# Start of a two-layer fp32 kernel: bias rows and modulation rows moved into the empty expert ring, the bias store moved to the first attention, the modulation's second part spread over the attention's units

## The reference, cut to what matters

```python
# second block, layer l; hc is the context, h the tokens that the first block gives
mod_c = (silu(c_ctx) @ w_mod[l] + b_mod[l])         # 6 rows of 1024; the same for c
cn = rms_norm(hc, norm1_g[l]) * (1 + mod_c[1]) + mod_c[0]
pc = cn @ w_in[l]                                   # q, k, v, pool, conv, gates
oc = diff_attn_core(qc, kc, vc, lam)                # 8 heads, 256 tokens: "attention 0"
hc = hc + mod_c[2] * mixer_output(oc, pc, ...)      # gates, pooling, convolution, w_out
cn2 = rms_norm(hc, norm2_g[l]) * (1 + mod_c[4]) + mod_c[3]
hc = hc + mod_c[5] * peer_ffn(cn2, ...)             # rows of 16384 experts, gathered
# first block, layer ab: s = q k^T + bias[bucket(distance)], bias from rel_bias (32 x 16)
```

## Time and profile before

| | |
|---|---|
| median of 3 runs | 4165.67 us |
| lowest and highest | 4165.25, 4172.52 us |
| span of the profiled execution (the page gives no other time of it) | 4175.5 us |
| PE, DVE, POOL busy | 50%, 67%, 45% of the span |
| mean granted TensorE clock | 0.734 of full speed |
| chain that ended last, by engine | PE 37%, DVE 27%, POOL 15%, issue 9%, DMA 7% |

### The profile page before, as it was taken

One profiled execution on the slowest core, in us unless ns is written; L12 is line 12 of the kernel. 1 busy time (PEld: TensorE's weight loads), 2 busy tenths in 40 slices (PEclk: granted clock), 3 DMA queues, 4 the chain that ended last, 5 costly groups with the idle time before them and its releaser, 6 DMA issues.

```text
span 4175.5 us, 29452 instructions
## 1 busy us (share of the span) xinstructions
PE 2101.5 (50%) x10122; PEld 1670.6 (40%) x10122; DVE 2787.7 (67%) x4546; ACT 414.1 (10%) x915; POOL 1893.4 (45%) x1556
## 2 busy tenths in 40 slices
PE   2798998637678578869435000009899800000000
PEld 0546887536467356767114000007688700000000
DVE  0104113996877997766987888994511399898898
ACT  0103001111311220011001000001400100000000
POOL 0000000355654776540875777770000057778776
PEclk7897999868788679989767555559999955555555
DMA  9552455779998989987998999993144557999999
GB/s 118 155 182 92 142 186 186 249 246 349 332 333 294 330 306 369 373 325 237 373 344 324 392 350 374 372 345 130 43 151 156 172 185 258 334 378 342 375 374 347
DMA packets 533813, 1140.12 MB, mean 273 GB/s; under 512 B 38125, under 2 KB 327789, under 8 KB 532878
## 3 DMA queue, kind: packets, MB, share of 16 engines
q0 software_dynamic: 224832, 814.87, 54.5%
q1 hardware_dynamic: 308832, 323.37, 23.6%
HBM read 1130.67 MB, written 7.44 MB: 273 GB/s over the span
## 4 chain that ended last, share of the span: by engine, by line
PE 37%; DVE 27%; POOL 15%; issue 9%; DMA 7%; ACT 2%; another core or an unknown queue 2%; SPq 0%; DVEq 0%; ACTq 0%; POOLq 0%
PE PS L399 35%; POOL ring L919 15%; DVE acc L1269 11%; DVE ring L1263 6%; DMA wring<-in_w_in 2%; DMA wring<-in_w_mod 1%; DMA ring<-in_peer_u,eidx 1%; ACT work L947 1%; DVE work L1323 1%; DVE work L1716 1%; DVE work L1714 1%; DVE work L1713 1%; PE PS L655 1%; DVE work L1329 1%
## 5 line engine op out<-in xcount | busy, mean ns | idle before, releaser
L919 POOL DMA_INDIRECT ring<-in_peer_u,eidx x768 | 996.9, 1298 | 1817.0 <-DVE small L1369 751.6
L919 POOL DMA_INDIRECT ring<-in_peer_v,eidx x768 | 885.3, 1153 | 431.4 <-issue 208.4
L1269 DVE SCALAR_TENSOR_TENSOR acc<-ring,small,acc 128x1024 f32<-128x1024 f32 x762 | 977.6, 1283 | 78.8 <-DMA ring<-in_peer_v,eidx 15.5
L1263 DVE SCALAR_TENSOR_TENSOR ring<-ring,xn_peer 128x1024 f32<-128x1024 f32 x768 | 930.5, 1219 | 122.4 <-DMA ring<-in_peer_u,eidx 114.1
L399 PE MATMUL PS<-wring,xnT 128*128 128x256 f32 (+1 forms) x3360 | 749.2, 387 | 43.9 <-issue 35.1
L399 PEld LDWEIGHTS PS<-wring,xnT 128*128 128x128 f32 x3360 | 651.2, 196 | 140.0 <-issue 40.9
L399 PE MATMUL PS<-xnT,wring 128*128 128x128 f32 (+1 forms) x2896 | 482.1, 329 | 30.6 <-DMA wring<-in_w_in 15.0
L399 PEld LDWEIGHTS PS<-xnT,wring 128*128 128x128 f32 x2896 | 439.8, 195 | 71.9 <-DMA wring<-in_w_in 16.6
L407 PE MATMUL PS<-const,work 128*128 128x128 f32 (+1 forms) x358 | 60.4, 334 | 744.6 <-DVE work L1326 681.0
L407 PEld LDWEIGHTS PS<-const,work 128*128 128x128 f32 (+1 forms) x358 | 52.0, 170 | 753.2 <-DVE work L1326 685.8
L947 ACT ACTIVATE work<-PS 128x512 f32<-128x512 f32 (+7 forms) x391 | 201.6, 535 | 1392.9 <-PE PS L399 1144.6
(11 more groups left out here) (151 smaller groups left out, 1484.9 us busy)
## 6 DMA issues: line engine op xcount, KB each, us to landing
wring<-in_w_in SPq DMA_DIRECT2D x128, 1024.0 KB
wring<-in_w_mod SPq DMA_DIRECT2D x48, 1024.0 KB
wring<-in_peer_wq SPq DMA_DIRECT2D x48, 1024.0 KB
wring<-in_ab_w_in SPq DMA_DIRECT2D x13, 1024.0 KB
wring<-in_conv_out_w SPq DMA_DIRECT2D x12, 1024.0 KB
wring<-in_w_out SPq DMA_DIRECT2D x12, 1024.0 KB
ring<-in_peer_u,eidx POOLq DMA_INDIRECT x768
ring<-in_peer_v,eidx POOLq DMA_INDIRECT x768
```

The lines of the kernel that those rows point to most:

```text
L919: pool.indirect_dma_start(ring[:, m % NG, :], None, table, bass.IndirectOffsetOnAxis(ap=eidx[:, r % 2, t, k:k + 1], axis=0))\
L1263: v.scalar_tensor_tensor(out=slot, in0=slot, scalar=1.0, in1=xn_peer[:, t, :], op0=ALU.mult, op1=ALU.mult, accum_out=hid[:, k:k + 1]).then ...
L1269: v.scalar_tensor_tensor(out=acc[:, :], in0=slot, scalar=wgt[:, k - NSEL:k - NSEL + 1], in1=acc[:, :], op0=ALU.mult, op1=ALU.add).then_inc ...
```

## The change

`MODROW` of layer 0, `hot` and `brow` move from `work` to `ring`, so that nothing of mixer 0 lies under them. The constants are split: the pooling matrices come as their own load, on SP ahead of the block ("mod0_1", 0), with a semaphore of their own, for which PE waits before the pooling. `modulation(0, 1)` is no longer called in one piece: PE runs one of its 8 units after the scores of each odd unit of attention 0, and ACT copies its rows in the next step. POOL waits for the first scores of attention 0, then loads `x`, then stores the bias rows. SP loads the norm row and the first two q blocks ahead of the first `mod_out`, and the second `mod_out` moves from g0 to u. ACT's waits for `bias_stored` and `mod_stored` go; POOL gets one for `mod_stored` ahead of the experts. ACT copies `xnT` ahead of the exponentials of lambda.

```diff
-        MODROW = [[work[0:2, b:b + 2 * D] for b in base] for base in ((0, 8192, 14336), (0, 2048, 4096))]
-        hot = work[0:33, 12288:13312].rearrange("p (g j) -> p g j", g=2)
-        brow = work[0:8, 13312:14336].rearrange("p (g j) -> p g j", g=2)
+        early = ring[:, :, :].rearrange("p n d -> p (n d)")
+        MODROW = [[early[0:2, b:b + 2 * D] for b in (0, 2048, 4096)], [work[0:2, b:b + 2 * D] for b in (0, 2048, 4096)]]
+        hot = early[0:33, 6144:7168].rearrange("p (g j) -> p g j", g=2)
+        brow = early[0:8, 7168:8192].rearrange("p (g j) -> p g j", g=2)
...
-            def attention(s, units, scores, turns, values):
+            def attention(s, units, scores, turns, values, between=None):
...
                         done(ins, "S", s, u)
+                        if between:
+                            between(u)
...
-                qkv(r, "qkv", (lambda: modulation(0, 1)) if r == 0 else None)
+                qkv(r, "qkv")
...
-                attention(r, M_UNITS, scores, turns, values)
+                def modulate(u):
+                    if u % 2:
+                        modulation(0, 1, u // 2)
+
+                attention(r, M_UNITS, scores, turns, values, modulate if r == 0 else None)
...
+                pe.wait_ge(poolm_landed, 16)
                 for c in range(0, KD, 2):
...
-            sp.dma_start(const[:, :], DR["const"]).then_inc(const_landed, 16)
+            sp.dma_start(const[:, 0:C_POOL], DR["const"][:, 0:C_POOL]).then_inc(const_landed, 16)
...
+            def load_pool_matrices():
+                sp.dma_start(const[:, C_POOL:C_ALL], DR["const"][:, C_POOL:C_ALL]).then_inc(poolm_landed, 16)
...
-                ("q0", 0): [(mod_out, 0, 0, 1), (load_rows, "n1_0", "sc_0", "sh_0", "ag_0"), (load_smalls, 0)],
-                ("g00", 0): [(mod_out, 0, 1, 3), (load_rows, "ps_0", "m2_0")],
+                ("q0", 0): [(load_rows, "n1_0")],
+                ("q0", 2): [(mod_out, 0, 0, 1), (load_rows, "sc_0", "sh_0")],
+                ("k0", 0): [(load_smalls, 0), (load_rows, "ag_0")],
+                ("mod0_1", 0): [(load_pool_matrices,)],
+                ("u0", 0): [(mod_out, 0, 1, 3), (load_rows, "ps_0", "m2_0")],
...
-            pool.dma_start(H["x"][:, :, :], DR["x"][0].rearrange("(t p) d -> p t d", p=P)).then_inc(x_landed, 16)
             slow(cT[:, :, 0], DR["c_2"][0].rearrange("(k p) -> p k", p=P), c_landed)
...
+            pool.wait_ge(*at("product", "S", 0, 0))
+            pool.dma_start(H["x"][:, :, :], DR["x"][0].rearrange("(t p) d -> p t d", p=P)).then_inc(x_landed, 16)
             for g in range(2):
                 pool.wait_ge(*at("read", "bias", g))
...
             pool.wait_ge(bias_stored, 32)
+            pool.wait_ge(mod_stored, 48)
...
-                if r == 0:
-                    act.wait_ge(bias_stored, 32)
                 for n in names:
...
-                    if r == 0 and n == "v":
-                        modulation(0, 1)
...
-                if r == 0:
-                    act.wait_ge(mod_stored, 48)
...
                 norm(("m", r), H[s], before)
+                norm_turn(("m", r))
                 if r in (0, 3):
                     act.wait_ge(*at("lam_dots", r))
                     A(act.activation(lam2[:, :], lam2[:, :], ACT.Exp), "lam_exp", r)
-                norm_turn(("m", r))
...
                 for u in range(len(M_UNITS) + 2):
+                    if r == 0 and u and u % 2 == 0:
+                        modulation(0, 1, 4 + u // 2 - 1)
```

More of the change, by code:

```diff
@@ L41 @@
 C_FREQ = C_IOTA + 16
-C_POOL = C_FREQ + 16
-C_ONES = C_POOL + 4 * T * S
-C_ALL = C_ONES + 2
+C_ONES = C_FREQ + 16
+C_POOL = C_ONES + 2
+C_ALL = C_POOL + 4 * T * S
 def constants():
@@ L62, in constants @@
     c[:, C_IOTA:C_IOTA + 16] = np.arange(16)
-    c[:, C_ONES:C_ALL] = 1.0
+    c[:, C_ONES:C_POOL] = 1.0
     c[:, C_FREQ:C_FREQ + 16] = 10000.0 ** (-np.arange(0, C_ROPE, 2) / C_ROPE)
@@ L248, in program @@
         freq = const[:, C_FREQ:C_FREQ + 16]
-        poolm = const[:, C_POOL:C_ONES].rearrange("p (i t s) -> p i t s", i=4, t=T)
+        poolm = const[:, C_POOL:C_ALL].rearrange("p (i t s) -> p i t s", i=4, t=T)
         O_TOK, PROB = wk(10240, T, D), [wk(12288, 1024), wk(13312, 1024)]
@@ L301, in program @@
         slot_used = sem("expert_rows_used")
-        const_landed = sem("const_landed")
+        const_landed, poolm_landed = sem("const_landed"), sem("pool_matrices_landed")
         x_landed, ctx_landed = sem("x_landed"), sem("ctx_landed")
@@ L457, in _, with modulation @@
             pe.wait_ge(*at("silu_c"))
-            def modulation(l, part):
+            def modulation(l, part, only=None):
                 for n in range(0, 16 if part else 8, 2):
+                    if only not in (None, n // 2):
+                        continue
                     pair = [weights(f"mod{l}_{part}", n + j) for j in range(2)]
@@ L467, in modulation @@
                         ins = sumk(PS[0:2, b, j * WB:(j + 1) * WB],
-                                   [(cT[:, kk, :], w[:, kk, :]) for kk in range(KD)] + [(const[0:1, C_ONES:C_ALL], bias)])
+                                   [(cT[:, kk, :], w[:, kk, :]) for kk in range(KD)] + [(const[0:1, C_ONES:C_POOL], bias)])
                     done(ins, "mod", l, m)
@@ L621, in first_block, with qkv @@
                 project_out("c", "c_out")
-            def qkv(r, names, then=None):
+            def qkv(r, names):
                 for n in names:
                     tokens(f"{n}{r}", 4, xnT, (n, r))
-                if then:
-                    then()
                 for n in names:
@@ L1106, in first_block, with modulation @@
                 norm("final", H["x"], [("h_c",)])
-            def modulation(l, part):
+            def modulation(l, part, only=None):
                 for n in range(12)[4:] if part else range(4):
+                    if only not in (None, n):
+                        continue
                     act.wait_ge(*at("product", "mod", l, n))
```

## The result

The changed kernel took 4120.28 us (median of 4 runs, 4118.69 to 4122.37), the kernel before 4165.46 us beside it: a ratio of 0.9895, 95% interval 0.9879 to 0.991, so 37 to 50 us faster, 45.2 between the medians. I had predicted 4151 us, 14 us faster, with a range from 4124 to 4180. The direction was right; the gain was three times the predicted one and the time lies 4 us under the range.

What follows compares the result with a forecast made beforehand. PE's chain of work bounds the front, with a stall from the bias store. Start -80.1, q -2.1, attention with modulation +67.9 sum to -14.3 us: 4165.67 becomes 4151 us, range 4124 to 4180.

Steps and rivals of the forecast that it cites:

- last copy of the first modulation: At the start, without the store's stall, the copy ends at 55.7 us instead of 135.8: gain 80.1 us.
- from there to q: From that copy to the first q product, reordered loads and `xnT` copies save 2.1 us of 21.0, bounds 1.0 and 3.0.
- first scores to the store's issue: In attention 0, scores start at 248.2 and POOL issues the store at 251.0, in old times.
- store's issue to PE's restart: In attention 0, PE restarts 93.4 us after the store's issue, at 344.4 in old times, as before the change.
- third modulation unit: Right after PE's restart in attention 0, at half clock at first: 8.2 + 2.7 = 10.9 us.
- five groups: Rest of attention 0: five times two attention units and one modulation unit, 16.9 us each, 84.5 us in all.
- tail to g0: Behind the last modulation unit, 6.9 us remain to the first g0 product, as before.
- The stall in attention 0: At step 5 PE waits about 56 us for the third modulation unit's blocks, held back by the store.
- Slower rival: Clock stays down in attention 0's third modulation unit and groups: 33 us more, 4184 us; chance 0.08.
- slipping weights: Weights get through during the store in attention 0, so the 56 us wait goes: 4095 us; chance 0.05.
- catch of the second unit's blocks: In attention 0 the store delays these blocks too, one more 16.9 us group behind the restart: 4168 us; chance 0.14.
- fast-clock case: Clock stays up through attention 0's groups, 12.8 us each: 20.5 us less, 4131 us; chance 0.15.

Runs made afterwards that it cites:

- experiment 1: (`mod_block`) Changed kernel with the 8 modulation units in one piece behind v again, so attention 0 runs alone beside the store: 4082.77 us, ratio 0.9812.
- experiment 5: (`wide_block`) Changed kernel with the bias store through 128 partitions and the modulation in one piece behind v: 4069.04 us, ratio 0.9818.
- experiment 6: (`wide_four`) Changed kernel with the bias store through 128 partitions and two modulation units at every fourth attention unit: 4052.77 us, one run.
- experiment 3: Changed kernel with bias rows loaded broadcast into 128 partitions and stored from there: 4033.08 us, ratio 0.9708; repeated 4048.08 us, ratio 0.9711.
- mod_block_wait: Changed kernel, modulation in one piece behind v, and ACT again waiting for the stored modulation rows before copying q and k: 4090.98 us, one run.

## Why the prediction was right or wrong

The chain of causes was right: the stall left the start, stood again in attention 0 and cost less there. What was wrong is what the clock does in the five groups behind it. From its forecast of 14.3 us to the 51.0 us at g0:

| step of the prediction | predicted | measured | less |
|---|---|---|---|
| last copy of the first modulation | 55.7 | 53.6 | 2.1 |
| from there to q | 18.9 | 17.0 | 1.9 |
| first scores to the store's issue | 2.8 | 1.8 | 1.0 |
| store's issue to PE's restart | 93.4 | 87.1 | 6.3 |
| third modulation unit | 10.9 | 9.4 | 1.5 |
| five groups | 84.5 | 63.1 | 21.4 |
| tail to g0 | 6.9 | 4.9 | 2.0 |

That is 36.2 of the 36.7 us; the other 0.5 lie in q, k, v and the copies behind them.

- **The groups are the step that failed.** I took 16.9 us, "each group to lose the clock in the attention units and win it back in the modulation", as 8.2 + 2.5 + 6.2, of which the 2.5 and the 6.2 have no row of their own; the belief came from two rows: the pause of 1.62 us after which the clock fell at 261 us, and the attention that never rose. The measured 12.62 us are the bound at full clock that I had worked out as 12.8, and had given a chance of 0.15. Experiments 1, 5 and 6 show why: sparse attention does lose the clock, but straight behind dense modulation it ran 8 us or more at 1.00, and a group has 4.5 us of it. The row at 261 us was one pause with no work in it, and attention before had started at 0.50; neither shows what attention does straight behind dense work. The tail and part of the third unit are the same error.
- **The stall in attention 0** was forecast at about 56 us ending near 262 and was 64.1 us ending at 250.35: it began earlier, since PE reached step 5 sooner, at full clock. The restart came 87.1 us behind the store's issue, not 93.4. Over the eight profiles it is 85.0 to 87.3 in five and 91.6 to 93.4 in three; what tells the two apart stays open.
- **The start and q** were each 2 us too small in the first profile. The start's 2 us are no clear error: in the second profile of the changed kernel the last copy ends at 56.3 us, 0.6 later than forecast. `x` costs 3.7 to 4.6 us where I took 3, with a bound of 3.8. The stretch from the copy to q shrank by 4.0 us where I took 2.1, with a bound of 3.0.
- **Slower rival, slipping weights, catch of the second unit's blocks:** none happened. The modulation unit in step 3 started without a wait, and in no run did the blocks that PE waited for land before the narrow store was over. The prediction set this against the Trainium skill's rule (DMA: Bandwidth & Descriptors, Queues, rings and completion order) that each DMA engine takes turns between its queues packet by packet. That was a wrong reading: the traces agree with the rule (492 and 492 packets, experiment 3), and the restart at 116.13 us doesn't speak against it. What doesn't follow from it is that the blocks arrive 9.8 us after their issue, since the store's packets last 1.18 us and those of the weights 0.05.
- **The spreading's own worth** I had put at nothing ("nothing of a modulation unit hides, for both are PE's"). That is so, and yet it is worth 24.6 us without the stall, through the clock. With the store beside it the spreading is a loss, since the modulation is what needs weights then (experiment 1).
- **The range** was missed by 4 us because the fast-clock case, at 4131, was its lower end with 7 us to spare, and that case also takes the 11 to 13 us by which start, q and restart were too pessimistic. The total shows less than the front: 45.2 us between the medians against 51.0 at g0, within the scatter of what follows.

## What to carry to other kernels

Moving a slow transfer moves its stall: it pays only as much as the new place has work whose operands have already landed, so look for what asks for data there, and first ask why the transfer is slow. Read there how many packets each queue moved and how long one took, for two queues that take turns packet by packet don't share the time evenly. Here a broadcast into 128 partitions ahead of the store removed the stall (ratio 0.971 instead of 0.9895). When dense PE work is spread into a sparse, latency-bound stage, cost the stage at both clocks and give the two cases like chances, unless a row shows how long such sparse work keeps the clock. Count a shift at a landmark behind the edit (here the first gather, 51.5 us), since the rest of this program alone scattered by 33 us.

## What the runs showed of the hardware that I had not expected

- Straight behind 16 us of modulation, attention ran at clock 1.00 for 8 us, PE busy for 5.62 and 5.89 of them, then fell to half in two of three stretches (`wide_four`). Where pauses of 1.8 and 1.7 us stood at its start, it was at half clock within 4 us (`mod_block`, `wide_block`). Started at half clock it did not rise in 57 us (`mod_block_wait`).
- 4 MB from 8 partitions: 82.7 us to landing, 0.53 MB in 10 us beside 0.13 MB of weights; 4 MB from 128 partitions in the same 2 KB pieces, with 4 MB of loads and the weights beside it: 355 GB/s in all.
- Two DMA queues took turns packet for packet (389 and 388 in 30 us), while one of them had 95.7% of the engines' time and the other 3.7%.
- Halves of the narrow store, issued apart, held weights back for 49.4 and 51.6 us each, against 87.1 us for the whole. One half alone used 47% of the engines' time at nearly the rate of both.
